# Gate and up projection of a SwiGLU layer: seven half-size Strassen products in place of eight, with h stationary and the weights moving

## The reference, cut to what matters

```python
def _rmsnorm(x, g):
    xf = x.astype(jnp.float32)
    y = xf * lax.rsqrt(jnp.mean(xf * xf, axis=-1, keepdims=True) + EPS)
    return (y * g.astype(jnp.float32)).astype(x.dtype)

def _swiglu(h, w_gate_up, w_down):
    gu = h @ w_gate_up
    return (jax.nn.silu(gu[..., :D_FF]) * gu[..., D_FF:]) @ w_down

        x = x + _swiglu(_rmsnorm(x, ffn_norm[layer]), ffn_w_gate_up[layer], ffn_w_down[layer])
```

## Time and profile before

| | us |
|---|---|
| median of 3 runs | 1296.13 (1295.98 to 1296.76) |
| profiled execution, first to last instruction (span) | 1294.5 |
| first FFN: first group / other ten groups / down | 22.7 / 217.0 / 119.8 |
| second FFN: first group / other ten groups / down | 27.9 / 217.2 / 121.0 |

### The profile page before, as it was taken

One profiled execution on the slowest core, in us unless ns is written; L12 is line 12 of the kernel. 1 busy time (PEld: TensorE's weight loads), 2 busy tenths in 40 slices (PEclk: granted clock), 3 DMA queues, 4 the chain that ended last, 5 costly groups with the idle time before them and its releaser, 6 DMA issues.

```text
span 1294.5 us, 18372 instructions
## 1 busy us (share of the span) xinstructions
PE 1282.6 (99%) x6525; PEld 1028.3 (79%) x6525; DVE 561.9 (43%) x872; ACT 551.6 (43%) x1006; POOL 611.3 (47%) x487
## 2 busy tenths in 40 slices
PE   8999999999999999999999999999999999999998
PEld 6877787877778888888888887777888888888886
DVE  4855666666535512121202056999843131311011
ACT  5454454445435433333323247785533233333223
POOL 4565664646535454545444453430444444444442
PEclk9999999999999999999999999999999999999999
DMA  6522222222233333333332345224323333343322
GB/s 210 160 73 62 68 68 58 66 57 67 89 97 111 96 98 97 97 96 94 102 95 85 106 126 175 66 68 152 98 82 91 104 90 105 89 122 98 97 95 93
DMA packets 123415, 126.31 MB, mean 98 GB/s; under 512 B 7896, under 2 KB 106456, under 8 KB 122712
## 3 DMA queue, kind: packets, MB, share of 16 engines
q1 hardware_dynamic: 123320, 125.46, 32.3%
q10 hardware_dynamic: 32, 0.01, 0.0%
HBM read 119.15 MB, written 6.29 MB: 97 GB/s over the span
## 4 chain that ended last, share of the span: by engine, by line
PE 65%; issue 19%; POOL 10%; DVE 3%; ACT 2%; DMA 1%; POOLq 0%; SPq 0%; ACTq 0%; DVEq 0%
PE ps L1518 19%; PE ps L1520 18%; PE ps L1519 18%; POOL w_lo L502 10%; PE ps L1896 2%; PE ps L1613 1%; PE ps L1625 1%; PE ps L1636 1%; PE ps L1671 1%; PE ps L1648 1%; PE ps L1652 1%; PE ps L1682 1%; PE ps L1690 1%; DMA x_tok<-in_x_dram 1%; DVE gelu_g L1426 0%
## 5 line engine op out<-in xcount | busy, mean ns | idle before, releaser
L502 POOL TENSOR_TENSOR w_lo<-w_stage,w_hi 128x512 fp32r<-128x512 f32 (+2 forms) x430 | 545.6, 1274 | 667.5 <-ACT w_hi L562 667.2
L562 ACT ACTIVATE w_hi<-w_stage 128x512 fp32r<-128x512 f32 (+2 forms) x448 | 264.5, 594 | 569.6 <-PE ps L1520 551.7
L1518 PE MATMUL ps<-h_hi,w_hi 128*128 128x512 f32 x1104 | 439.7, 398 | 1.7 <-DVE h_lo L955 1.0
L1520 PE MATMUL ps<-h_hi,w_lo 128*128 128x512 f32 x1104 | 430.5, 390 | 0.0
L1519 PE MATMUL ps<-h_lo,w_hi 128*128 128x512 f32 x1104 | 430.4, 390 | 0.0
L1518 PEld LDWEIGHTS ps<-h_hi,w_hi 128*128 128x128 f32 x1104 | 207.4, 188 | 61.1 <-issue 14.2
L1520 PEld LDWEIGHTS ps<-h_hi,w_lo 128*128 128x128 f32 x1104 | 207.3, 188 | 43.7
L1519 PEld LDWEIGHTS ps<-h_lo,w_hi 128*128 128x128 f32 x1104 | 207.5, 188 | 43.2 <-issue 2.6
L1301 DVE TENSOR_TENSOR silu_g<-ps,rstd_wide 128x512 f32<-128x512 f32 x44 | 30.2, 686 | 327.5 <-PE ps L1520 327.5
L1518 PE MATMUL ps<-w_hi,f_hi 128*128 128x512 f32 x176 | 68.7, 390 | 0.1
L1519 PE MATMUL ps<-w_lo,f_hi 128*128 128x512 f32 x176 | 68.5, 389 | 0.0
(11 more groups left out here) (229 smaller groups left out, 1634.3 us busy)
## 6 DMA issues: line engine op xcount, KB each, us to landing
w_stage<-in_ffn_w_gate_up_dram SPq DMA_DIRECT2D x176, 256.0 KB, 3.1
w_stage<-in_ffn_w_down_dram SPq DMA_DIRECT2D x88, 256.0 KB, 2.7
w_stage<-in_even_w_in_dram SPq DMA_DIRECT2D x96, 192.0 KB, 2.5
w_stage<-in_odd_w_in_dram SPq DMA_DIRECT2D x32, 256.0 KB, 2.8
x_spill<-x_t SPq DMA_DIRECT2D x2, 2048.0 KB, 8.6
x_t<-x_spill SPq DMA_DIRECT2D x2, 2048.0 KB, 9.3
w_stage<-in_odd_w_out_dram SPq DMA_DIRECT2D x16, 256.0 KB, 2.8
w_stage<-in_even_w_out_dram SPq DMA_DIRECT2D x16, 192.0 KB, 2.4
```

The costliest lines, as they stand in the source:

```text
L502: pool.tensor_tensor(out=w_lo[:, s, 0:n], in0=stage[:, s, 0:n], in1=w_hi[:, s, 0:n].bitcast(f32), op=ALU.subtract).then_inc(chunk_lo, 1)
L562: act.activation(w_hi[:, j % RING, 0:n], stage[:, j % RING, 0:n], ACT.Copy).then_inc(chunk_hi, 1)
L1518: pe.matmul(out_, lh, rh, start=start, stop=False, skip_group_check=skip)
L1520: return pe.matmul(out_, ll, rh, start=False, stop=stop, skip_group_check=skip)
```

## The change

The first 256 of each 2816 gate and up columns are still computed plainly (8 chunks), now token-major: `h` is stationary, the 512 weight columns move. The other 2560 are five units of 512 gate and 512 up columns. With tokens split in halves, the 1024 input features in halves and gate against up, a unit is a 2 x 2 by 2 x 2 block product, made by seven products p1 to p7 (Strassen's scheme in Winograd's form) instead of eight. A product is 4 chunks, and a chunk serves 2 token tiles (6 matmuls) instead of 4.

- Sums of weights: four per unit and row block (`sum7`, `sum5`, `sum6`, `sum3`), in place, by VectorE. The raw weights are loaded as 512 x 512 blocks (1 MB) into six buffers A to F.
- Sums of h: `mix_sums` (16 operations of 128 x 256 per FFN), with their high part on ScalarE and low part on VectorE (`mix_low`), from `h_gained`, a copy of x times the gain (8 per FFN).
- Low parts in the units: VectorE makes chunks 0, 1 and 2 of each product (`low`, semaphore `unit_lo`), GpSimd chunk 3.
- Products accumulate on one another in PSUM where the scheme allows; ScalarE copies three of them out (`first_copy`, `second_copy`, `fifth_copy`), VectorE adds.
- f comes out token-major. TensorE transposes it back: `turn_f`, 4 transposes for each of the 22 blocks of f, four blocks ahead of the down projection, which must then split f into high (ScalarE) and low (VectorE) parts.
- The norm's factor is now one number per token, on 128 x 8 instead of 128 x 512.
- The Fori loops of the FFN are gone on all engines; everything is written out.

```diff
+RAW = ("g1", "g2", "u1", "u2")
+RAW_OF = {"p1": "g1", "p2": "g2", "p4": "u2", "p5": "u1", "p6": "u1", "p3": "g2", "p7": "g1"}
+SUM_OF = {"p7": 0, "p5": 1, "p6": 2, "p3": 3}
+def unit_products(u):
+    before = [("p4", u - 1)] if u else []
+    if u == UNITS - 1:
+        return [("p1", u)] + before + [(name, u) for name in ("p5", "p6", "p2", "p7", "p3", "p4")]
+    return [("p2", u), ("p1", u)] + before + [(name, u) for name in ("p5", "p6", "p3", "p7")]
+PRODUCTS = [step for u in range(UNITS) for step in unit_products(u)]
+PRODUCT_AT = {step: e for e, step in enumerate(PRODUCTS)}
+UNIT_CHUNKS = 4 * len(PRODUCTS)
...
+                def mix_sums(j):
+                    dve.wait_ge(h_gained_in, KD * n + 2 * j + 2)
+                    if j >= 2:
+                        dve.wait_ge(mix_hi_done, 4 * n + j - 1)
+                        dve.wait_ge(mix_lo_done, 4 * n + j - 1)
+                    near, far = h_gained[:, j % 2, 0, :], h_gained[:, j % 2, 1, :]
+                    into = h_sum[:, j % 2, :, :]
+                    done = 4 * (4 * n + j)
+                    V.tensor_tensor(into[:, 0, :], near[:, HT:T], near[:, 0:HT], ALU.subtract).then_inc(h_summed, 1)
+                    V.tensor_tensor(into[:, 2, :], far[:, HT:T], near[:, HT:T], ALU.subtract).then_inc(h_summed, 1)
+                    dve.wait_ge(h_summed, done + 1)
+                    V.tensor_tensor(into[:, 1, :], far[:, HT:T], into[:, 0, :], ALU.subtract).then_inc(h_summed, 1)
+                    dve.wait_ge(h_summed, done + 3)
+                    V.tensor_tensor(into[:, 3, :], far[:, 0:HT], into[:, 1, :], ALU.subtract).then_inc(h_summed, 1)
+                def mix_low(j):
+                    dve.wait_ge(mix_hi_done, 4 * n + j + 1)
+                    dve.wait_ge(h_summed, 4 * (4 * n + j + 1))
+                    V.tensor_tensor(h_mix[:, :, j, 1, :], h_sum[:, j % 2, :, :], h_mix[:, :, j, 0, :].bitcast(f32), ALU.subtract)\
+                     .then_inc(mix_lo_done, 1)
...
+                def low(name, u, k):
+                    c = unit_chunk(n, name, u, k)
+                    dve.wait_ge(chunk_hi, c + 1)
+                    s = c % RING
+                    V.tensor_tensor(w_lo[:, s, :], unit_source(n, name, u, k), w_hi[:, s, :].bitcast(f32), ALU.subtract).then_inc(unit_lo, 1)
...
+                def sum7(u, k):
+                    low_read("p1", u, k)
+                    g1, u1 = raw("g1", u, k), raw("u1", u, k)
+                    V.tensor_tensor(g1, g1, u1, ALU.subtract).then_inc(w_summed, 1)
...
+                def multiply(name, u):
+                    done = 2 * (UNITS * n + u)
+                    if name == "p2" and u == 0:
+                        pe.wait_ge(norm_sqrt, nn)
+                    elif name == "p2":
+                        pe.wait_ge(gate_early_in, done)
+                    if name == "p1" and u < 2:
+                        pe.wait_ge(plain_f, NC * n + 2 * (u + 1))
+                    elif name == "p1":
+                        pe.wait_ge(f_early_done, done - 2)
+                    if name == "p5" and u == 0:
+                        pe.wait_ge(mix_lo_done, 4 * (n + 1))
+                        if n == 1:
+                            pe.wait_ge(x_tok_in, NC)
+                    elif name == "p5":
+                        pe.wait_ge(gate_late_in, done)
+                    if name == "p6":
+                        pe.wait_ge(first_out, done + 2)
+                    if name == "p3":
+                        pe.wait_ge(fifth_out, done + 2)
+                    if name == "p7":
+                        pe.wait_ge(second_out, done + 2)
+                    if name == "p4":
+                        pe.wait_ge(up_late_in, done + 2)
+                    bank = {"p2": other, "p5": other + 2, "p3": other + 2}.get(name, fb + 2 * (u % 2))
+                    for k in range(4):
+                        c = unit_chunk(n, name, u, k)
+                        chunk_ready(c)
+                        s = c % RING
+                        for m in range(2):
+                            rh, rl = tokens_of(name, k, m)
+                            last = mm3(ps[:, bank + m, :], rh, rl, w_hi[:, s, :], w_lo[:, s, :], name in ("p1", "p2", "p5") and k == 0, k == 3, True)
+                        last.then_inc(chunk_used, 1)
+                def turn_f(k):
+                    if k < 2:
+                        pe.wait_ge(f_early_done, 2 * (UNITS * n + last_unit))
+                    else:
+                        pe.wait_ge(f_lo_done, KF * n + k - 1)
+                        pe.wait_ge(f_early_done, 2 * (UNITS * n + (k - 2) // 4 + 1))
+                        pe.wait_ge(f_late_done, 2 * (UNITS * n + (k - 2) // 4 + 1))
+                    for c in range(NC):
+                        last = pe.transpose(ps[:, fb + 2 + k % 2, c * P:(c + 1) * P], f_tokens(k, c), ident[:, :])
+                    last.then_inc(f_turned, 1)
...
+                    for d in range(KF - 3 * g):
+                        if g == 0 and d + 4 < KF:
+                            turn_f(d + 4)
+                        ready(d)
+                        for m in range(4):
+                            last = tile(d, m)
+                        last.then_inc(chunk_used, 1)
```

More of the change, by code:

```diff
@@ L72, in loaded @@
 def loaded(c):
-    return 16 * (c // RING + 1)
+    n = sum(c >= C_FFN[n] + GROUP_CHUNKS + UNIT_CHUNKS for n in range(2))
+    return 16 * ((c - UNIT_CHUNKS * n) // RING + 1)
 def width(c):
@@ L391, in rows @@
                 return slice(k * P, (k + 1) * P)
-            def plain(c0, w, col, k_tiles=KD, first=0):
-                for k in range(first, k_tiles):
-                    load(c0 + k, c0 + k, stage[:, (c0 + k) % RING, :], w[rows(k), col:col + 512])
             sync.dma_start(ident[:, :], A["consts"][:, K_IDENT:K_IDENT + P]).then_inc(consts_in, 16)
@@ L835, in _ @@
+            ffn(0, 1, G_MIX + 8, 0)
             second_half(2, G_MIX + 8, C_ODD)
@@ new lines, in ffn @@
+                low("p5", last, 2)
+                sum6(last, 0)
+                sum6(last, 1)
+                low("p6", last, 0)
+                sum6(last, 2)
+                low("p6", last, 1)
+                sum6(last, 3)
+                low("p6", last, 2)
+                late_f(last - 1, 0)
+                late_f(last - 1, 1)
+                low("p2", last, 0)
+                low("p2", last, 1)
+                low("p2", last, 2)
+                early_f(last - 1, 0)
+                early_f(last - 1, 1)
@@ new lines, in ffn @@
+                low("p4", last, 0)
+                f_low(1)
+                low("p4", last, 1)
+                low("p4", last, 2)
+                late_gate(last, 0)
+                late_gate(last, 1)
+                f_low(2)
+                late_f(last, 0)
+                late_f(last, 1)
+                f_low(3)
+                early_f(last, 0)
+                early_f(last, 1)
+                for k in range(4, KF):
+                    f_low(k)
+                    if k == KF // 2 and n == 0:
+                        softplus_out()
@@ L1792, in ffn, with group @@
                 c0 = C_FFN[n]
[L1794 to L1798 removed]
+                other, last_unit = 4 - fb, UNITS - 1
+                def group():
                     for k in range(KD):
[L1800 to L1801 removed]
+                        c = c0 + k
+                        if k == NORM_SUM_AT:
```

684 lines of the change are left out of this document (511 added, 173 removed).

## The result

| | us |
|---|---|
| changed kernel, median of 4 runs | 1273.07 (1272.80 to 1273.15) |
| before, 4 runs beside it | 1296.45 (1295.98 to 1297.83) |
| ratio | 0.9816, 95% interval 0.9802 to 0.9830 |
| span of the profiled execution | 1271.3 (before 1294.5) |

What follows compares the result with a forecast made beforehand. The number of 512-column matmuls on TensorE was taken to bound the FFNs. Terms -54.3 + 19.2 + 3 + 3.4 + 7.3 + 1 = -20.4 us gave 1274.1 from 1294.5, about 1276 us as median, range 1262 to 1300.

Steps and rivals of the forecast that it cites:

- Matmuls, -54.3: Gate and up of both FFNs: 240 fewer 512-column matmuls at 0.2263 us each, -54.3 us.
- Transposes, +19.2: Down projections: 176 added TensorE transposes of f at 0.109 us each, +19.2 us; 20.9 if something is paid per group.
- Steady units, +3: Later units: TensorE 38.0 us, VectorE 35.9, smallest margin of a low 0.6 to 0.8; +0.4 for each of 8 units.
- Unit 0, +3.4: First unit of each FFN: without p4 between p1 and p5, lows come late, +1.7 us per FFN.
- the first FFN's start, +1: Start of the first FFN's units: ScalarE is the late one, second low 0.6 us late; +1 us, from 0 to 4.
- The hole, 5.9 + 0.4: Second FFN ahead of p2 of unit 0: TensorE waits for lows behind VectorE's queue, 5.9 us plus 0.4 for the second.
- rival (c): Behind the hole 8 to 16 matmuls run slow, +2 to +4 us, plus 5 from other waits: 1280 to 1291; 14%.
- Norm sum and loads, nothing: The norm's 512-column matmul becoming four of 2 columns, and waits on 1 MB weight loads, were both counted as nothing.
- The end, +1: Last unit and down projection: `turn_f` placement and `softplus_out` between f blocks on VectorE, +0.5 us each.
- (a): Every unit: VectorE becomes the bound at 41.7 us per unit, slower than before, about 1306, typical 1302; 18%.
- (b): Starts of the units are covered too and units have no wait: 1261 to 1266 us; 14%.
- (d): Transposes of f cost double, a full switch each way per group of 4: +18 us, 1294, no change; 4%.

Runs made afterwards that it cites:

- rep_k0: Changed kernel with the first chunk's matmuls of p1, p2 and p5 issued twice in every unit, 180 matmuls more; 1310.57 us.
- turn2: Changed kernel with every transpose of f issued twice, 176 transposes more; 1291.38 us.
- low7: Changed kernel with one more VectorE subtraction per product, 7 per unit, ahead of the first low, result unread; 1289.99 us.
- fill_hole: Changed kernel with 26 matmuls, results unread, put ahead of p2 of unit 0 in the second FFN, where TensorE waited; 1271.50 us.
- copies_on_act: Changed kernel with the second FFN's four token copies moved from VectorE to ScalarE, and the first high part of h behind a conversion; 1267.94 us.
- start3: Like copies_on_act, but in ScalarE's order the fourth copy stands later and the last two high parts of h each ahead of a conversion; 1266.28 us.

## Why the prediction was right

- *Matmuls, -54.3.* Right. 0.2263 us each in steady units; rep_k0 shows that more of them cost their time.
- *Transposes, +19.2.* Measured 21.0, which was the upper case that I had named (20.9, with something paid per group of four). I took the value of eight in a row, but 36 of 44 groups stand alone. The 0.109 for one was good (0.107 in turn2).
- *Steady units, +3.* Measured 0. The sum for VectorE was too high by 4 us because every one of GpSimd's lows was charged 1.1 us, 7.7 in all; only a meeting with operations that have both operands in SBUF costs, two of seven do, and they cost 2.0. (Operations that don't stand back to back take 0.68 us, not the 0.60 counted, which gives a part back.) The Trainium skill (GPSIMD Engine Reference, Specifications) names that condition for contention, and the rows at 999.87 and 1005.19 agree. The smallest margin of 0.6 to 0.8 us was nevertheless of the right kind: low7 shows that 0.6 us more per product is too much.
- *Unit 0, +3.4, and the first FFN's start, +1.* Measured 2.0 in the first FFN together (2.7 predicted); in the second no wait of unit 0 is seen, since TensorE comes later there; in fill_hole, where it doesn't, there are 2.1 us of waits.
- *The hole, 5.9 + 0.4.* Measured 6.2 with VectorE's `w_lo` as releaser, right in place, size and cause; copies_on_act and start3 remove it by removing what stood ahead.
- *Slow matmuls behind it.* Not in the sum, but rival (c), at +2 to +4 for 8 to 16 matmuls: it came, twelve matmuls and 2.7 us, and its place was taken by the terms that fell away. I had left it out since no row of before showed it mid-kernel; the earlier trace rows were the nearest, though without a lower clock beside them, and on them it got 14%. The rows at 941.45 to 946.91 now show it: 0.43 us apart at clock 0.50 after 6.2 us of standing still. As a term of the sum it was 2.7, as a price of the hole only about 0.5, as fill_hole shows. The Trainium skill (TensorE: Matmul & The Clock Gate, Why this matters for your kernels) says that a pause between bursts brings the clock back to half, and the trace agrees.
- *Norm sum and loads, nothing.* Right. The eight small matmuls take 0.9 us, as did the two of 512 columns before; no wait on a raw load.
- *The end, +1.* No hole was found there, and the account closes without it.

Terms for waits were 14.7 together and measured 10.2 (2.0 + 6.2 + 2.7 - 0.7); the transposes were 1.8 low. Net, the span fell 2.8 us more than predicted. What bounds the kernel, what the change removes and where the one large hole stands were right, and the runs show them; that the total came within 3 us is in part luck, since 2.7 us that the sum left out stand against 7.2 of waits that it had too many. (A small slip: the hop of 0.07 us is 0.08 by the rows named for it; nothing hangs on it.) Of the rivals, (a) was avoided by the 2.5 us per unit that low7 measured, (b) by VectorE's copies, and (d) is shown wrong by the 0.485 us per group and by turn2.

## What to carry to other kernels

A scheme that trades matmuls for sums is worth its matmuls as long as no low comes late; the busy share of the engine that makes the sums doesn't tell this (VectorE had 6.4 us free per unit and could use 2.5 at the place tried), a walk through its queue with durations from the trace does. Look for the price at the seams, where one stage's leftovers stand in an in-order queue ahead of the next stage's first operand: here 8.9 us lay at one such place, and moving four copies and reordering one queue brought back 6.9. A hole of several us on TensorE brings slow matmuls behind it, but their price is only what wasn't cover for the next wait: here 0.5 of 2.7 us, so it is the hole's cause that is worth removing, not the low clock. And an operation handed to GpSimd is not free for VectorE.
